# Interleaving eight modulation-weight chunks with the chunks of the input projection

## The reference: what is computed

```python
def trunk_layer(x, cvec, lw, gla_s0, k_ctx, v_ctx):
    sh1, sc1, g1, sh2, sc2, g2 = split(silu(cvec) @ w_ada + b_ada, 6)     # w_ada: 1024 x 6144
    h = rms_norm(x, norm_mix) * (1 + sc1) + sh1
    gq, gk, gv, gg, glr, conv_in, nq, nk, nv = split(h @ w_in)            # w_in: 1024 x 2848
    mix = concat(gated_linear_attention(gq, gk, gv, gg, glr),
                 conv_module(conv_in), neighbourhood_attention(nq, nk, nv)) @ w_out
    x = x + g1 * mix
    h = rms_norm(x, norm_ffn) * (1 + sc2) + sh2
    return x + g2 * moe(h)                                                # 64 experts, top 8, one shared
```

## Time and profile before

| | us |
|---|---|
| median of 3 runs | 1731.21 (1730.26 to 1733.71) |
| profiled execution, whole time | 1729.89 |
| profiled execution, its span | 1728.2 |
| mean granted TensorE clock (share of full) | 0.939 |
| PE busy | 1503.5 (87% of the span) |
| DVE, ACT, POOL busy | 449.8, 294.4, 171.0 |
| input projection, layer 0 and layer 1 | 84.0, 83.9 |
| from there to GLA's first decays, layer 0 and 1 | 47.6, 48.0 |

### The profile page before, as it was taken

The page is one execution under the profiler, slowest core; times in us unless marked ns, Lnnn a source line. Parts: engine busy times, 40 slices in busy tenths (PEclk is TensorE's granted clock), DMA queues, the critical chain, the costliest instruction groups (busy, mean ns, idle before and its releaser), DMA issues. The chain is left out here.

```text
span 1728.2 us, 28448 instructions
## 1 busy us (share of the span) xinstructions
PE 1503.5 (87%) x12136; PEld 804.5 (47%) x12137; DVE 449.8 (26%) x867; ACT 294.4 (17%) x485; POOL 171.0 (10%) x357
## 2 busy tenths in 40 slices
PE   4897888699998989899849979888998899999994
PEld 3655665544443434344337567564343333433431
DVE  1261674511111111111134318543111111111111
ACT  2313212411110101011013231233111001110110
POOL 3550330200000000000003206101000000000000
PEclk8998989799999999999979989889999999999997
DMA  7648910099999999999645495004999999999992
GB/s 250 231 139 314 334 45 6 1 367 412 378 415 388 421 385 420 373 421 406 288 138 194 155 386 222 7 1 173 382 414 389 421 385 397 417 404 388 399 421 109
DMA packets 109252, 509.56 MB, mean 295 GB/s; under 512 B 12864, under 2 KB 14652, under 8 KB 59196
## 3 DMA queue, kind: packets, MB, share of 16 engines
q1 hardware_dynamic: 108508, 506.52, 73.4%
q0 software_dynamic: 384, 1.05, 0.3%
q10 hardware_dynamic: 224, 0.06, 0.0%
HBM read 505.49 MB, written 2.10 MB: 294 GB/s over the span
## 5 line engine op out<-in xcount | busy, mean ns | idle before, releaser
L909 PE MATMUL ps<-ring,h 128*32 128x512 f32 x3328 | 388.9, 621 | 67.6 <-DMA ring<-in_exp_w_up 42.3
L909 PEld LDWEIGHTS ps<-ring,h 128*32 128x32 f32 x3328 | 118.2, 114 | 332.9 <-issue 332.6
L928 PE MATMUL ps<-ring,mid 128*32 128x512 f32 x1664 | 200.1, 598 | 3.1 <-DVE hT L1504 1.6
L935 PE MATMUL ps<-hT,mid 128*128 128x512 f32 x416 | 192.4, 605 | 1.6 <-DVE hT L1512 1.6
L895 PEld LDWEIGHTS ps<-tm,mid 128*128 128x128 bf16 x2496 | 144.4, 98 | 44.3 <-issue 43.1
L895 PE MATMUL ps<-tm,mid 128*128 128x128 bf16 x2496 | 156.9, 219 | 0.3
L1502 DVE TENSOR_TENSOR mid<-mid,ps 128x256 f32<-128x256 f32 x52 | 21.9, 422 | 464.7 <-ACT mid L1203 464.7
L935 PEld LDWEIGHTS ps<-hT,mid 128*128 128x128 f32 x416 | 74.7, 189 | 120.0 <-issue 116.5
L1504 DVE COPY hT<-ps 128x512 f32<-128x512 f32 x52 | 36.0, 692 | 328.9 <-PE ps L928 328.9
L1203 ACT ACTIVATE mid<-ps 128x256 f32<-128x256 f32 x52 | 20.0, 384 | 528.9 <-PE ps L909 528.9
L1593 POOL TENSOR_TENSOR ring<-ring,maskr 128x512 f32<-128x512 f32 x2 | 45.0, 22482 | 630.5 <-DMA ring<-in_cache_na_v 630.5
(11 more groups left out here) (279 smaller groups left out, 1298.2 us busy)
## 6 DMA issues: line engine op xcount, KB each, us to landing
ring<-in_exp_w_gate SPq DMA_DIRECT2D x128, 1024.0 KB, 10.9
ring<-in_exp_w_up SPq DMA_DIRECT2D x128, 1024.0 KB, 13.1
ring<-in_exp_w_down SPq DMA_DIRECT2D x128, 1024.0 KB, 14.1
ring<-in_w_ada SPq DMA_DIRECT2D x28, 2048.0 KB, 13.4
ring<-in_w_in SPq DMA_DIRECT2D x6, 2048.0 KB, 9.6
ring<-in_w_out SPq DMA_DIRECT2D x4, 2048.0 KB, 7.8
ring<-in_w_in SPq DMA_DIRECT2D x2, 3072.0 KB, 10.5
ring<-in_w_in SPq DMA_DIRECT2D x2, 2176.0 KB, 10.6
```

The lines of the kernel that those rows point to most:

```text
L909: last = mm(ps[first:first + TILE, 4, :], X_e[:, b, kt, first:first + TILE], gate_up(ring[:, slot, :], kt), start=(kt == 0), stop=(kt == K ...
L928: last = mm(ps[first:first + TILE, 7, :], turn[:, P * j + first:P * j + first + TILE], down(ring[:, slot, :], j, half), start=(j == 0), st ...
L935: last = mm(bank(2 * st + half), turn[:, FF + P * st:FF + P * (st + 1)], Y[:, 512 * half:512 * (half + 1)], start=False, stop=False, skip_ ...
```

## The change

The order of the 20 loads becomes a list, in which eight of the modulation chunks stand between those of the input projection; `AT` gives a chunk's number. TensorE multiplies them in the same places (`ADA_BEHIND`), ScalarE copies them there, and their banks and waits are adapted. From step 8 on, numbers, slots and places are those of before. The small loads now go with n = 2, which is still the second input chunk. The new order of n:

in0, ada0, in1, ada1, ada2, in2, ada3, ada4, in3, ada5, ada6, in4, ada7, ada8, ..., ada11, out0, out1, shared.

```diff
+CHUNKS = ([("in", 0), ("ada", 0), ("in", 1), ("ada", 1), ("ada", 2), ("in", 2), ("ada", 3), ("ada", 4), ("in", 3),
+           ("ada", 5), ("ada", 6), ("in", 4), ("ada", 7)] + [("ada", m) for m in range(8, ADA_CHUNKS)]
+          + [("out", half) for half in range(OUT_CHUNKS)] + [("shared", 0)])
+AT = {chunk: n for n, chunk in enumerate(CHUNKS)}
+PRE = len(CHUNKS)
-ADA_EARLY = 5
+ADA_IN = 8
+ADA_BEHIND = [[m for m in range(ADA_IN) if AT["in", c] < AT["ada", m] < AT.get(("in", c + 1), PRE)]
+              for c in range(len(IN_CHUNKS))]
...
-                if n == 1:
+                if n == 2:
...
-                if n == C_ADA - 1:
+                if (kind, m) == ("in", len(IN_CHUNKS) - 1):
                     sp.wait_ge(s["h_ready"], STREAMS)
...
         def ada_bank(m):
-            return bank(m % 2 if m < ADA_EARLY else 4 + m % 2 if m < ADA_GLA else 5, 0, P)
+            return bank(4 if m == 0 else m % 2 if m < ADA_IN else 5, 0, P)
...
-                pre_loaded(pe, C_ADA + m)
-                if m == 0:
+                pre_loaded(pe, AT["ada", m])
+                if m == 1:
                     pe.wait_ge(s["la_ready"], STREAMS)
-                elif m == ADA_EARLY + 1:
-                    pe.wait_ge(s["cat_conv"], 1)
-                elif m > ADA_GLA:
+                elif m > ADA_IN:
                     pe.wait_ge(s["ada_kept"], m)
-                elif m != ADA_EARLY and m > 1:
+                elif 2 < m < ADA_IN:
                     pe.wait_ge(s["ada_kept"], m - 1)
...
+                if u in LAST_UNIT:
+                    for m in ADA_BEHIND[LAST_UNIT.index(u)]:
+                        ada_step(m)
...
             last.then_inc(s["convT_shown"], 1)
-            for m in range(3):
-                ada_step(m)
             pe.wait_ge(s["ctok_ready"], 1)
...
             last.then_inc(s["convB_shown"], 1)
-            ada_step(3)
-            ada_step(4)
             pe.wait_ge(s["cact_ready"], 1)
...
             last.then_inc(s["nT_shown"], 1)
-            ada_step(5)
             pe.wait_ge(s["nT_ready"], 1)
...
-            ada_step(6)
-            ada_step(7)
             pe.wait_ge(s["p_ready"], 1)
-            pe.wait_ge(s["ada_kept"], ADA_EARLY)
+            pe.wait_ge(s["ada_kept"], ADA_IN)
```

More of the change, by code:

```diff
@@ L429, in chunk_used @@
     def chunk_used(eng, n):
[L431 to L436, removed]
+        kind, i = CHUNKS[n]
+        if kind == "in":
+            eng.wait_ge(s["proj_done"], LAST_UNIT[i] + 1)
+        elif kind == "ada":
+            eng.wait_ge(s["ada_done"], i + 1)
+        elif kind == "out":
+            eng.wait_ge(s["mix_shown"], 2 * (i + 1))
         else:
@@ L457, in _ @@
                 sem = chunk_in[pre_slot(n)]
-                if C_ADA <= n < C_OUT:
-                    m = n - C_ADA
+                kind, m = CHUNKS[n]
+                if kind == "ada":
                     dma_in(sp, ada_weights(pre_slot(n)), ada_columns(layer, ADA_FIRST + m) if m < ADA_LATER else
                            ada_columns(following, m - ADA_LATER), sem)
-                elif n < C_ADA:
-                    c0, cw = IN_CHUNKS[n]
+                elif kind == "in":
+                    c0, cw = IN_CHUNKS[m]
                     dma_in(sp, slot[:, 0:KT * cw].rearrange("p (k n) -> p k n", k=KT),
                            A["w_in"][layer, :, c0:c0 + cw].rearrange("(p k) n -> p k n", k=KT), sem)
-                elif n < C_SH:
-                    c0 = 512 * (n - C_OUT)
+                elif kind == "out":
+                    c0 = 512 * m
                     dma_in(sp, slot[:, 0:KT * 512].rearrange("p (k n) -> p k n", k=KT),
@@ L613, in ada_step @@
             def ada_step(m):
-                pre_loaded(pe, C_ADA + m)
-                if m == 0:
+                pre_loaded(pe, AT["ada", m])
+                if m == 1:
                     pe.wait_ge(s["la_ready"], STREAMS)
-                elif m == ADA_EARLY + 1:
-                    pe.wait_ge(s["cat_conv"], 1)
-                elif m > ADA_GLA:
+                elif m > ADA_IN:
                     pe.wait_ge(s["ada_kept"], m)
-                elif m != ADA_EARLY and m > 1:
+                elif 2 < m < ADA_IN:
                     pe.wait_ge(s["ada_kept"], m - 1)
-                ada_product(ada_weights(pre_slot(C_ADA + m)), ada_bank(m)).then_inc(s["ada_done"], 1)
+                ada_product(ada_weights(pre_slot(AT["ada", m])), ada_bank(m)).then_inc(s["ada_done"], 1)
             modulation(0)
@@ L631, in _ @@
                 if u == 0 or UNITS_IN[u - 1][0] != c:
-                    pre_loaded(pe, c)
+                    pre_loaded(pe, AT["in", c])
                 if u >= len(PROJ_BANKS):
@@ L635, in _ @@
                 cw = IN_CHUNKS[c][1]
-                wt = ring[:, pre_slot(c), 0:KT * cw].rearrange("p (k n) -> p k n", k=KT)[:, :, c0:c0 + w]
+                wt = ring[:, pre_slot(AT["in", c]), 0:KT * cw].rearrange("p (k n) -> p k n", k=KT)[:, :, c0:c0 + w]
                 b = PROJ_BANKS[u % len(PROJ_BANKS)]
@@ L809, in mix @@
             def mix(half, st, tiles):
-                w = ada_weights(pre_slot(C_OUT + half))
+                w = ada_weights(pre_slot(AT["out", half]))
                 for kt in tiles:
@@ L816, in _ @@
             for half in range(2):
-                pre_loaded(pe, C_OUT + half)
+                pre_loaded(pe, AT["out", half])
                 if half == 1:
@@ L860, in _ @@
             last.then_inc(s["counted"], 1)
-            shared = ring[:, pre_slot(C_SH), :]
+            shared = ring[:, pre_slot(AT["shared", 0]), :]
             pe.wait_ge(s["shared_in"], 48)
@@ L1084, in _ @@
                     nc.scalar.activation(csig, ci[:, 2:4, :], ACT.Sigmoid).then_inc(s["conv_sig"], 1)
+                if u in LAST_UNIT:
+                    for m in ADA_BEHIND[LAST_UNIT.index(u)]:
+                        keep_ada(m)
             rsqrt_act(act, link, N_CONV, numbers(N_CONV, 1), numbers(N_CONV, 2))
-            for m in range(3):
-                keep_ada(m)
             act.wait_ge(s["convB_shown"], 1)
@@ L1100, in _ @@
                                  ACT.Sigmoid).then_inc(s["gg_sig"], 1)
-            keep_ada(3)
-            keep_ada(4)
             act.wait_ge(s["pw_shown"], 1)
@@ L1109, in _ @@
             nc.scalar.copy(kcT, bank(6, 0, 256).rearrange("p (a n) -> p a n", a=2)).then_inc(s["nT_ready"], 1)
-            keep_ada(5)
             for st in range(STREAMS):
@@ L1121, in _ @@
                 last.then_inc(s["p_exp"], 1)
-            keep_ada(6)
-            keep_ada(7)
             act.wait_ge(s["pT_shown"], 1)
```

## The result

The changed kernel took 1795.99 us (median of 4 executions, 1792.0 to 1801.8) against 1732.46 us for the kernel before (4 executions): a ratio of 1.036, 95% interval 1.034 to 1.039, or 63.5 us more. The forecast was 1784 us with a range of 1768 to 1794: the sign and the mechanism came out, the size did not.

The account below looks back on a forecast made before the run. TensorE was taken to bound the input projection and loads the stage behind it. Per layer 37.0 added less 10.0 gained gave +27.0 us, +54 for two on 1729.9: 1784 us, range 1768 to 1794.

Parts of the forecast that it names:

- eight products: Input projection: eight moved modulation products of 1.9 us each lie on TensorE's path, 15.2 us a layer.
- waits for weights: Input projection: in2, in3 and in4 land late, covered by only two modulation products; stalls 4.5, 7.1, 4.5, together 16.1 us.
- clock loss behind them: Input projection: TensorE runs at a lower clock after each of three stalls, 1.9 us each, 5.7 a layer.
- stage behind the projection: From the projection to GLA's first decays: load waits leave, gaining 10.0 us a layer; bounds 14.6 and 8.4.
- The queue will be idle: Input projection: modulation chunks ahead have landed when an input chunk is issued, so 2 MiB lands in 8.0 us.
- cover of 2.7 us for ada2: Input projection: ada2 lands by 938.7 and TensorE wants it at 941.4, so no wait.
- the chain: Behind the projection: dependent steps through the engines bound the stage once load waits leave, 33.4 us against 48.0.
- The list of what runs slower: Behind the projection: step 8, twelve transposes, pointwise convolution and its transposes lose 4.1 to 6.2 us; 4.6 taken.
- the small loads were in time: Second rival, 7%: small loads land late in the projection and TensorE stands within in0; 5 us a layer, 1794.
- the clock did not keep up: First rival, 10%, claimed the clock keeps up behind the projection: full 14.6 us gained, 22.4 a layer slower, 1775.
- the loads were not hidden: Third rival, 4%, claimed the projection's loads are hidden: no stalls or clock loss, +0.6 us a layer, 1731.
- The fourth rival: Clock stays down through the second stage and the start of GLA: some 5 us a layer more, 1793; 6%.

Follow-up runs that it names:

- run 3: The changed kernel, with each modulation load behind an input chunk issued only once that chunk had landed: 1799.5 us, ratio 1.039.
- run 4: The changed kernel plus filler products that nobody reads while TensorE waits for the third, fourth and fifth input chunks: 1788.7 us, ratio 1.034.
- run 10: The changed kernel with the ring turned by two slots, so input chunks from slot 2 lie in slot 1: 1806.5 us, ratio 1.042.
- run 11: The kernel before with the ring turned by one slot, its last input chunk going to slot 2: 1762.3 us, one execution.
- run 7: The kernel before with only two modulation chunks moved, each input chunk issued a whole input product ahead: 1720.9 us, ratio 0.994.
- run 1: The changed kernel with the third input chunk in idle buffers outside the ring, the fourth issued when the second is used: 1774.5 us, ratio 1.024.
- run 6: The changed kernel plus filler products that nobody reads in the three long waits behind the projection: 1797.6 us, ratio 1.037.
- run 12: The changed kernel executed again, unchanged, for a second profile: 1799.1 us, ratio 1.039.
- Run 5: The changed kernel with third and last input chunks in places outside the ring and the fourth issued ahead of two modulation loads: 1755.6 us, ratio 1.015.
- Run 8: The kernel before with three modulation chunks moved, each input chunk issued a product ahead: 1719.1 us, ratio 0.992.

## Why the prediction was wrong in size

Per layer, the prediction's terms and what the profiles have (first profile, layer 0 / layer 1):

| term | predicted | measured |
|---|---|---|
| eight products | +15.2 | +15.0 |
| waits for weights | +16.1 | +18.4 / +19.2 |
| clock loss behind them | +5.7 | +6.2 / +7.2 |
| stage behind the projection | -10.0 | -10.6 / -7.1 |
| rest (stage lengths less the rows above) | | +1.1 / +0.5 |
| sum | +27.0 | +30.0 / +34.8 |

Over both layers that is some 11 us more than the 54 predicted. The waits are 5.4 of it, the clock behind them 2.0, the stage behind the projection 2.3, the rest 1.6, and the products took 0.4 less.

**Ring and waits: right in place, mis-sized.** The step that failed is "on an idle queue a w_in chunk of 2 MiB lands 8.0 us after its issue". It was taken from one row, the only one of its kind with an idle queue, and the upper bound allowed 0.4 us for all three waits together (16.5 for 16.1); in the changed kernel the same load lands in 9.1 to 9.6 us, so the waits are 18.4 and 19.2. The landings in layer 1, of the third, the fourth and the last input chunk:

```profile
ring<-in_w_in SPq DMA_DIRECT2D x1, 2048.0 KB, 9.6
...
ring<-in_w_in SPq DMA_DIRECT2D x1, 3072.0 KB, 10.7
...
ring<-in_w_in SPq DMA_DIRECT2D x1, 2048.0 KB, 9.2
```

The landing of 10.6 for 3 MiB was right (10.5 and 10.7). The modulation load in the same group, 8.7, was a neighbour that would have carried the bound up. Landings of 8.0 us would take some 5 us off the measured time, which makes 1791, inside the range.

"The queue will be idle" did not hold for the third chunk: the modulation load ahead of it (ada2, landing 10.3 and 8.9 us after its issue) had 2.1 and 1.0 us still to go when it was issued. For the last chunk it held. What made that one slower than 8.0 is open: modulation loads issued behind it (run 3), an idle TensorE (run 4) and the slot (runs 10 and 11) are ruled out. One difference is left that no run was made to test, the time for which the DMA engines had moved nothing. Ahead of the last chunk of the changed kernel's layer 0 it is 12 us; the DMA share and the GB/s at the end of this row are 0:

```profile
141.50:153.30 11.80, 11.80 (x47) 7.12 (x49) 0.00 (x0) 1.08 (x3) 0.00 (x0) 1.00 0.00 0
```

In the kernel before and in runs 7 and 11 it is 0 to 2 us and the last chunk lands in 8.0 to 8.2 us; in the changed kernel and in runs 1, 3, 4, 6, 10 and 12 it is 9 to 14 us and the chunk lands in 9.1 to 9.7. That the two go together in the traces does not show that one causes the other.

The estimate from the Trainium skill, page "DMA: Bandwidth & Descriptors", of 6.8 and 9.2 us for the two sizes was further off than the rows; the runs show 8.0 to 9.7 for 2 MiB and 10.4 to 11.9 for 3 MiB. It took the higher of two rates: with the HBM limit of about 358 GB/s that stands beside the 435 in the page's section "Specifications" the same estimate would be 7.9 and 10.8 us. Those are close to the fastest landings seen, but the rate itself is not borne out as a limit: the stage behind the projection of the kernel before moved 366 and 368 GB/s on average.

**Products: right.** The cover of 2.7 us for ada2 was too large, it came just too late in layer 0: a wait of 0.4 us there and none in layer 1. Run 5 comes nearest to this term by itself: with its waits and their clock loss taken off, the stages are still some 12 us longer than before.

**Clock: right mechanism, low by 0.5 to 1.5 us.** "1.9 for each" came from gaps of 3 to 6 us; behind the waits here, of 5.2 to 7.2 us, 1.5 to 3.0 us were lost, 2.2 on average. Five of the six are above the 1.9 and four above the bound of 2.0. Run 4, in which the same products take 14.00, 20.91 and 14.00 us, shows that it is the clock.

**Second stage: the chain was right, its clock loss too small.** Run 8's 33.5 and 33.3 us are the 33.4 of the sum. The list of what runs slower left out the scores. They are many small products, took 4.7 us in the earlier trace rows (1013.37 on), and 7.1 in layer 1 of the changed kernel (1082.09 to 1089.15). With those 2.4 us the list comes to 6.5 to 8.6 and the gain to 6.0 to 8.1, which holds the 7.1 of layer 1 and the 6.7 and 7.1 of the second profile. In layer 0 of the first profile the scores came at the high clock (4.7 us) and the gain was 10.6. Which it is differs from profile to profile.

**Rivals.** No wait came at the place of L651 (the small loads were in time), the clock did not keep up, and the loads were not hidden. The fourth rival, the clock down through the second stage, is what layer 1 did, at 3 us and not 5. I gave it 6% as a case apart, though it only was the far end of the forecast's own term.

**Range.** With a landing of up to 9.6, a clock loss of up to 3 and the scores in the list, the high end would have been above 1800. The low end was built with more care than the high one.

## What to carry to other kernels

In a ring of n slots, write down for each load which load's use releases it: two heavy consumers exactly n apart have no prefetch between them, however many small ones stand there. Moving work out of a stage bound by loads pays only until that stage's own chain bounds it; here two or three of eight products did, and leaving the others in the chain's gaps also kept TensorE's clock up. A gain in one stage that is bought in a stage bound by the moved work's engine costs its full duration.

## What the runs showed of the hardware that was not expected

The last input chunk, 2 MiB of the same weights, took 8.0 to 8.2 us to land in some orders and 9.1 to 9.7 in others, the slower ones with the queue idle, by none of the causes tried. Turning the ring by one slot, with every load and product the same, cost 30 us through the first expert loads, which then had to wait for the shared expert's slot (run 11, one execution, was expected to take 1730). And the scores behind the projection ran at either clock in different layers and profiles of the same kernel (4.7 or 7.1 us). With them go the transposes ahead of them (1.3 or 1.9 us) and step 8 behind (2.6 or 3.5 us), which moves their stage between 37 and 41 us.
